# Two transformer blocks with expert layers: where the gate products stand in a round, and what ScalarE and VectorE do at the turn of a half

## The reference, cut to what matters

```python
def peer(x, w_q, sub_keys_1, sub_keys_2, u_tab, v_tab):
    ...
        q = (xb @ w_q).reshape(...)               # 8 heads, two parts each
        s1 = einsum('bthd,nd->bthn', q[..., 0, :], k1)   # 128 keys
        s2 = einsum('bthd,nd->bthn', q[..., 1, :], k2)   # 128 keys
        v1, i1 = top_k(s1, 16);  v2, i2 = top_k(s2, 16)
        top_s, pos = top_k(all sums of v1 and v2, 16)
        idx = i1 * 128 + i2 of those pairs        # one of 16384 experts
        g = softmax(top_s)
        h = einsum('bthkd,btd->bthk', u_tab[idx], xb)
        a = gelu(h) * g
        return einsum('bthk,bthkd->btd', a, v_tab[idx])
```

## Time and profile before

| | |
|---|---|
| median of 3 runs | 2250.28 us |
| the three runs | 2236.48, 2250.60, 2250.28 us |
| the profiled execution, its own time | 2250.24 us |
| its span in the profile | 2248.5 us |
| mean granted TensorE clock | 0.964 |
| PE busy | 2084.5 us, 93% |
| U stage, its gated half, block 1 | about 599 to 796 us |
| V stage, gated half, block 1 | about 800 to 1000 us |
| V stage, second half, block 1 | about 1008 to 1190 us |
| the same two turns in block 2 | at about 1840 and 2044 us |

### The profile page before, as it was taken

How to read it: one execution, slowest core, us unless ns; L and a number is a source line. 1 busy time by engine, 2 the same in 40 slices (tenths; PEclk the granted TensorE clock), 3 DMA queues, 4 the chain that set the end, 5 groups by cost and what they waited for, 6 DMA issues and landing times.

```text
span 2248.5 us, 41347 instructions
## 1 busy us (share of the span) xinstructions
PE 2084.5 (93%) x15340; PEld 1900.6 (85%) x15340; DVE 1239.6 (55%) x2076; ACT 976.5 (43%) x1206; POOL 1469.6 (65%) x592
## 2 busy tenths in 40 slices
PE   6898789998999999989997888999999999998997
PEld 6796789998999977768887868999999987776885
DVE  5547637992155556652334753996145556664333
ACT  3356344444444434434445453444444434443443
POOL 5654566798877767864445535699777768874442
PEclk9898899999999999999998989999999999999999
DMA  6332343444544444545555323445454445544553
GB/s 223 132 113 94 113 150 132 161 166 164 179 163 166 168 150 168 171 148 176 187 187 193 113 75 114 150 168 183 160 171 168 166 143 172 172 168 141 187 189 118
DMA packets 95823, 351.93 MB, mean 157 GB/s; under 512 B 11024, under 2 KB 11280, under 8 KB 95376
## 3 DMA queue, kind: packets, MB, share of 16 engines
q1 hardware_dynamic: 94752, 345.92, 45.9%
q10 hardware_dynamic: 1008, 5.13, 0.6%
HBM read 349.96 MB, written 1.05 MB: 156 GB/s over the span
## 4 chain that ended last, share of the span: by engine, by line
PE 76%; DVE 13%; POOL 4%; ACT 3%; issue 3%; DMA 1%; ACTq 0%; POOLq 0%; DVEq 0%; SPq 0%; PEldq 0%
PE ps L489 24%; PE ps L490 23%; PE ps L491 23%; POOL wlo L446 4%; PE ps L730 3%; DVE work L1347 1%; DVE work L1334 1%; PE ps L656 1%; DVE work L1327 1%; DVE work L1328 1%; DVE act L1171 1%; DVE whi L1103 1%; DVE act L1126 0%; DMA act<-in_const 0%; DVE act L1117 0%
## 5 line engine op out<-in xcount | busy, mean ns | idle before, releaser
L446 POOL TENSOR_TENSOR wlo<-ring,whi 128x1024 fp32r<-128x1024 f32 x588 | 1469.4, 2507 | 754.2 <-ACT whi L962 523.8
L962 ACT ACTIVATE whi<-ring 128x1024 fp32r<-128x1024 f32 x536 | 565.2, 1059 | 886.5 <-PE ps L491 841.2
L489 PE MATMUL ps<-hhi,whi 128*128 128x256 f32 x2432 | 701.1, 288 | 16.7 <-POOL wlo L446 15.3
L490 PE MATMUL ps<-hlo,whi 128*128 128x256 f32 x2432 | 692.2, 285 | 0.0
L491 PE MATMUL ps<-hhi,wlo 128*128 128x256 f32 x2432 | 691.8, 284 | 0.0
L489 PEld LDWEIGHTS ps<-hhi,whi 128*128 128x128 f32 x2432 | 471.3, 194 | 20.1 <-issue 11.6
L490 PEld LDWEIGHTS ps<-hlo,whi 128*128 128x128 f32 x2432 | 471.3, 194 | 0.0
L491 PEld LDWEIGHTS ps<-hhi,wlo 128*128 128x128 f32 x2432 | 470.7, 194 | 0.0
L489 PE MATMUL ps<-whi,shi 128*128 128x512 f32 x1024 | 413.8, 404 | 25.6 <-DVE slo L1430 25.6
L490 PE MATMUL ps<-wlo,shi 128*128 128x512 f32 x1024 | 408.6, 399 | 0.0
L491 PE MATMUL ps<-whi,slo 128*128 128x512 f32 x1024 | 407.6, 398 | 0.0
(11 more groups left out here) (241 smaller groups left out, 2029.3 us busy)
## 6 DMA issues: line engine op xcount, KB each, us to landing
ring<-in_weights SPq DMA_DIRECT2D x652, 512.0 KB, 3.3
act<-in_const SPq DMA_DIRECT2D x1, 2752.0 KB, 14.1
act<-in_const ACTq DMA_DIRECT2D x1, 2372.0 KB, 10.3
xres<-in_x SPq DMA_DIRECT2D x2, 512.0 KB, 4.4
act<-in_keys ACTq DMA_DIRECT2D x1, 1024.0 KB, 12.9
out<-act ACTq DMA_DIRECT2D x2, 512.0 KB, 2.6
act<-in_fgain ACTq DMA_DIRECT2D x1, 512.0 KB, 3.5
act<-in_keys SPq DMA_DIRECT2D x1, 128.0 KB, 13.8
```

The costliest lines, as they stand in the source:

```text
L446: pool.tensor_tensor(wlo[:, j, :], ring[:, j, :], whi[:, j, :].bitcast(F32), ALU.subtract)\
L489: pe.matmul(dst, wide[0], narrow[0], start=start, stop=False, skip_group_check=True)
L490: pe.matmul(dst, wide[0], narrow[1], start=False, stop=False, skip_group_check=True)
L962: eng.activation(whi[:, j, :], ring[:, j, :], ACT.Copy).then_inc(hi_ready[j], 1)
```

## The change

Three things. First, the gate products of a round follow tiles 0 and 2 (`EACH_GATED`), not 1 and 3; in the last round of each half they follow tiles 0 and 1 (`LAST_GATED`). Second, at the turn from U to V: ACT's last U round is written out, and `left(0, 0)` and `left(1, 1)` stand behind the rounding of place 2, ahead of the last gelu (now `open_pair(k, 2)`, which waits for `slot_used` of the last U tile) and of the rounding of place 3; DVE runs only one `hot` of the next half between the last two applies, and the other behind `rest_of(0, 0)` and `rest_of(1, 1)`; PE begins V's first tile with the second 128 tokens (t = 1, banks 2 and 3) and waits for the last gelu only ahead of t = 0. Third, in V's round 15 ACT's wait for `gates_used` of 64 stands behind the rounding of places 0 and 1, directly ahead of the `left` of pair 32. The sum that is computed is the same, and so is the number of all instructions but those of the waits and loops.

```diff
--- before.py
+++ after.py
@@ -72,6 +72,7 @@
 GATE_SCALE = 2.0 ** 14
 assert GROUPS == 2 * HALF_ROUND
 
+EACH_GATED, LAST_GATED = (0, 2), (0, 1)
 POOL_PLACES, DVE_PLACES = (0, 2), (1, 3)
 
 
@@ -731,14 +732,14 @@
                                            hot1[:, c, w, q, :], start=(q + w == 0), stop=(w == 1), skip_group_check=True)
                     mm.then_inc(n["gates_ready"], 1)
 
-                def u_round(k, first=False, gated=False):
+                def u_round(k, first=False, gate_after=()):
                     for j in range(RING):
                         pe.wait_ge(lo_ready[j], k + (first_u // RING + 1))
                         if j % 2 == 0 and not first:
                             pe.wait_ge(n["gelu_done"], k * 2 + (j // 2 - 1))
                         tile(j, bank(j // 2, (j % 2) * S, (j % 2 + 1) * S))
-                        if gated and j % 2:
-                            gates(k, -GROUPS, j // 2)
+                        if j in gate_after:
+                            gates(k, -GROUPS, gate_after.index(j))
 
                 u_round(0, first=True)
                 with pe.Fori(1, U_MID) as k:
@@ -753,31 +754,32 @@
                 mm.then_inc(n["selT_ready"], 1)
                 with pe.Fori(U_MID, HALF_ROUND) as k:
                     u_round(k)
-                u_round(HALF_ROUND, gated=True)
-                with pe.Fori(HALF_ROUND + 1, ROUNDS) as k:
-                    u_round(k, gated=True)
-
-
-                pe.wait_ge(n["gelu_done"], E_TILES // 2)
-
-                def v_round(k, first=False, last=False, gated=False):
+                u_round(HALF_ROUND, gate_after=EACH_GATED)
+                with pe.Fori(HALF_ROUND + 1, ROUNDS - 1) as k:
+                    u_round(k, gate_after=EACH_GATED)
+                u_round(ROUNDS - 1, gate_after=LAST_GATED)
+
+                def v_round(k, first=False, last=False, gate_after=()):
                     for j in range(RING):
                         pe.wait_ge(lo_ready[j], k + (first_v // RING + 1))
                         if j % 2 == 0:
                             pe.wait_ge(n["pair_ready"], k * 2 + (j // 2 + 1))
-                        for t in range(TT):
+                        for t in ((1, 0) if first and j == 0 else (0, 1)):
+                            if first and j == 0 and t == 0:
+                                pe.wait_ge(n["gelu_done"], E_TILES // 2)
                             for half in range(2):
                                 c, a = slice(half * 512, (half + 1) * 512), slice(t * P, (t + 1) * P)
                                 mm = split_product(bank(2 * t + half),
                                                    (shi[:, j // 2, j % 2, a], slo[:, j // 2, j % 2, a]),
                                                    (whi[:, j, c], wlo[:, j, c]), first and j == 0, last and j == RING - 1)
                         mm.then_inc(slot_used, 1)
-                        if gated and j % 2:
-                            gates(k, GROUPS, j // 2)
-
-                v_round(0, first=True, gated=True)
-                with pe.Fori(1, HALF_ROUND) as k:
-                    v_round(k, gated=True)
+                        if j in gate_after:
+                            gates(k, GROUPS, gate_after.index(j))
+
+                v_round(0, first=True, gate_after=EACH_GATED)
+                with pe.Fori(1, HALF_ROUND - 1) as k:
+                    v_round(k, gate_after=EACH_GATED)
+                v_round(HALF_ROUND - 1, gate_after=LAST_GATED)
                 with pe.Fori(HALF_ROUND, ROUNDS - 1) as k:
                     v_round(k)
                 v_round(ROUNDS - 1, last=True)
@@ -978,13 +980,16 @@
                                        bank(6 + (h - 1) % 2).rearrange("p (t c k) -> p t c k", t=TT, c=2), ACT.Copy)\
                            .then_inc(n["s_copied"], 1)
 
+                def open_pair(k, j):
+
+                    eng.activation(act[:, bass.ds(k * RING + j, 2), :], bank(j // 2).rearrange("p (e t) -> p e t", e=2),
+                                   gelu).then_inc(n["gelu_done"], 1)
+
                 def u_round(k):
                     for j in range(0, RING, 2):
                         high(first_u + j + RING, j, k)
                         high(first_u + j + 1 + RING, j + 1, k)
-
-                        eng.activation(act[:, bass.ds(k * RING + j, 2), :], bank(j // 2).rearrange("p (e t) -> p e t", e=2),
-                                       gelu).then_inc(n["gelu_done"], 1)
+                        open_pair(k, j)
 
                 def left(p, j):
 
@@ -998,23 +1003,32 @@
                 eng.activation(esel[:, :, 2, :, :].rearrange("p t h k -> p t (h k)"),
                                esel[:, :, 2, :, :].rearrange("p t h k -> p t (h k)"), ACT.Exp).then_inc(n["exp_ready"], 1)
                 eng.preload_act_table(gelu)
-                with eng.Fori(U_MID, ROUNDS) as k:
+                with eng.Fori(U_MID, ROUNDS - 1) as k:
                     u_round(k)
-
+                k = ROUNDS - 1
+                high(first_u + RING, 0, k)
+                high(first_u + 1 + RING, 1, k)
+                open_pair(k, 0)
+                high(first_u + 2 + RING, 2, k)
                 eng.wait_ge(n["gates_used"], GROUPS)
                 left(0, 0)
                 left(1, 1)
-
-                def v_round(k):
+                eng.wait_ge(slot_used, first_u + E_TILES)
+                open_pair(k, 2)
+                high(first_u + 3 + RING, 3, k)
+
+                def v_round(k, gated=0):
                     for j in range(RING):
                         high(first_v + j + RING, j, k)
+                        if j == 1 and gated:
+                            eng.wait_ge(n["gates_used"], gated)
                         if j % 2:
                             left(k * 2 + (2 + j // 2), j // 2)
 
                 with eng.Fori(0, HALF_ROUND - 1) as k:
                     v_round(k)
-                eng.wait_ge(n["gates_used"], 2 * GROUPS)
-                with eng.Fori(HALF_ROUND - 1, ROUNDS - 1) as k:
+                v_round(HALF_ROUND - 1, gated=2 * GROUPS)
+                with eng.Fori(HALF_ROUND, ROUNDS - 1) as k:
                     v_round(k)
                 split[0] = first_v + E_TILES
 
@@ -1421,7 +1435,7 @@
                 last_k = HALF_ROUND - 1
                 for c in range(2):
                     apply(last_k, c, 0, 0, c)
-                    hot(0, c, GROUPS, 1, c)
+                hot(0, 0, GROUPS, 1, 0)
                 eng.wait_ge(n["gates_used"], GROUPS)
 
                 def rest_of(p, j):
@@ -1438,6 +1452,7 @@
 
                 rest_of(0, 0)
                 rest_of(1, 1)
+                hot(0, 1, GROUPS, 1, 1)
                 eng.wait_ge(n["gelu_done"], E_TILES // 2)
                 with eng.Fori(0, HALF_ROUND - 1) as k:
                     for c in range(2):
```

## The result

The changed kernel takes 2215.32 us (median of 4 runs, 2208.03 to 2218.78) and the kernel before 2250.26. The ratio on record is 0.9864 with a 95% interval of 0.9819 to 0.9909; it is not the quotient of the two medians, which is 0.9845. By the medians the change takes 34.9 us less, where 32.8 were forecast (2217.4 us). Run to run, both kernels scatter by some 10 us. The profiles place it: PE starts on the first block's U tiles, after a wait for POOL, at 398.3 to 400.9 us in six of the thirteen profiled executions told of here and at 407.3 to 409.4 in the other seven, so most of the scatter comes from the first 400 us, which no edit here touches. Both kernels' main profiles are of the later kind (407.26 before, 409.02 after).

What follows compares the result with a forecast made beforehand. PE's own queue was taken to set the time, with gains only where PE stops at the turns. 22.0 (middle of V) + 10.8 (turn from U to V) = 32.8 us off 2250.2 gave 2217.4 us, range 2203 to 2228.

Steps and rivals of the forecast that it cites:

- The middle of V: Middle of V: PE's stop of 8.55 us and slow tile's 2.45 go, 11.0 us per block, 22.0 in all.
- The turn from U to V: Turn from U to V: PE's stop shrinks from 4.56 to 1.44 us, slow first tile goes; 10.8 us in two blocks.
- the step: At the turn, DVE's rest_of waits for POOL's low and ends at 4.27, so PE stands for 1.44 us.
- The clock: At the turn, PE's clock is kept after 1.44 us, winning 2.29; rival: it falls, 2222.0 us, chance 0.08.
- The lower bound of the middle's gain: Middle of V: at least 4.7 us won if a rest_of and one rounding stayed exposed and the clock fell.
- Gates after tiles 0 and 2: Inside the U and V halves: the earlier gates cost zero, as PE stays full.
- Almost no slack: Gated V rounds: DVE's loop just closes in one period of 6.07 us, yet rest_of is ready 1.8 ahead of PE.
- the slower rival: Gated V rounds: POOL takes the port twice running, PE stands 1.0 us each half round, 63 lost, 2280 us; chance 0.04.
- DVE's pace: Gated V rounds: DVE needs 6.36 us per half round, 0.29 over the period, 17.4 back, 2234.8 us; chance 0.06.
- No lock: At the turn, DVE gets its operands beside POOL, PE does not stand, 2 x 1.44 more won, 2214.5 us; chance 0.10.
- the middle in part: Middle of V: ACT holds a rounding back or a low waits, 4.7 us won of 11.0, 2230.0 us; chance 0.06.

Runs made afterwards that it cites:

- e1: The changed kernel with gates after tiles 1 and 3 again in all rounds except the last of each half; 2208.54 us, ratio to before 0.9841.
- e2: The changed kernel with the turn from U to V put back as in the kernel before, the middle of V staying changed; 2227.49 us, ratio 0.9913.
- e6: The changed kernel with ACT's wait for the last gates of V ahead of its whole round 15 again; 2222.98 us in one run.
- e7: The changed kernel with the gates of V's round 15 after tiles 1 and 3 again, ACT's wait staying as changed; 2210.0 us.
- e3: The changed kernel with ACT's gates wait and two pair roundings moved ahead of rounding weight place 2 in U's last round; 2207.18 us, ratio 0.9834.
- e4: The changed kernel with the low of weight place 2 at the turn made by DVE behind its two slo, not by POOL; 2214.86 us.
- e8: The changed kernel with two more DVE instructions of 0.60 us ahead of each gated one-hot of V; 2218.35 us in one run.
- e9: The changed kernel with four more DVE instructions of 0.60 us ahead of the one-hots in each gated V half round; 2268.41 us in one run.

## Why the prediction was right

**The bound.** PE's queue sets the time, and nothing inside a half was to be won: e1 shows it, and PE is full in 184 of 184 us.

**The middle of V, 22.0 us.** Shown. PE does not stop; e2 alone takes 12.2 + 11.0 = 23.2 us off the layers, 11.2 + 10.9 = 22.1 of them in V, where its edits are. The steps came as written: slo of pair 32 ended 3.25 us after the last gates' start (3.3 forecast) and that of pair 33 9.3 us after (9.1). What the prediction did not say is how the two edits share it; e6 and e7 do.

**The turn from U to V, 10.8 us.** The mechanism and nearly the size. PE stands for 1.60 us; the step put it at 1.44, since POOL began its low 1.40 after the end of tile 2 and not 1.33, and slo ended a little more behind it. The total difference to e2 is 3.6 + 6.8 = 10.4 us between the wide marks and 4.9 + 5.2 = 10.0 between the close ones, a little under the 10.8: the stop is 0.16 us longer than forecast, and the slow first tile took 4.84 us in e2's first block (791.56 to 796.40) and not 5.09, so there was less to win behind it. That POOL's instruction holds DVE's was read from one row of before; e3, e4 and e6 show it from three sides (slo moved, POOL's low removed, two of each made to meet).

**The clock.** Kept after 1.60 us, as taken; e6 and e7 add that it is kept after 2.93 and 2.82. The lower bound of the middle's gain had the clock fall for a stop of 3.9 us; no run stopped PE for a time between 2.93 and 4.56 at these turns, so that is open. The slow tiles behind the four stops are gone (2.87 us and not 5.09 at the turn).

**Gates after tiles 0 and 2, at no cost.** Right: 60 slo in the gated V rounds and the first at each turn took 2.3 to 2.4 us, DVE's time rose by 95.8 us, PE's did not. "Almost no slack" was too timid. e8 shows that another 1.2 us per half round fit, since a DVE that comes later waits less. A loss of about the size that the slower rival priced, 1.05 us per half round, does exist, and e9 shows it at 1.16. But it comes by the mechanism of the rival "DVE's pace", with about 2.4 us more DVE work; a POOL that takes its turn twice running was seen in none of the rows read here.

**The rivals.** "No lock" fell at the turn (1.60 us of stop and 2.99 us for two slo). "DVE's pace" and "the middle in part" left no stop to see. The mechanism was right, and that the median lies within 2 us of the forecast is in part luck, since whole runs scatter by 10. By layers it is 33.6 against 32.8, and in the stretches that the edits reach 32.1; the rest stands where nothing was edited.

**Which parts earn.** The last round's gates and ACT's order at the two turns: in the middle each was undone alone (e7, e6), at the turn from U to V only both together (e2), so how those two share their 10 us is not shown. The even places, the moved one-hot and the order of t are idle in this kernel; whether the last two would earn in e3, where PE comes sooner, was not tried.

## What to carry to other kernels

Where a long accumulation needs all of something before it can turn, look at the last round only: put its producers one or two tiles early and let the rest of the schedule be. Before moving a VectorE instruction with two SBUF inputs, lay GpSimd's instructions beside it: it costs its own length or about that plus the rest of GpSimd's, and an engine whose busy time is made of such waits is not full. To judge an edit worth 3 us in runs that scatter by 10, compare stretches between marks of the trace, and set the marks close around the edit.

## What the runs showed of the hardware

The granted clock of TensorE survived stops of 1.60, 2.82 and 2.93 us and was at its lower level behind stops of 4.56 and 8.55 us (0.51 to 0.52 of full speed over the first tile of before, 0.55 over that of e2, near whose end it had risen again). The stops up to 2.93 us cost only themselves; those of 4.56 us cost 2.0 to 2.3 us more.

The hold between POOL and DVE goes both ways and, in e6, by turns. slo took 0.68 us alone, 1.52 issued 1.4 us into POOL's low, 2.32 issued 0.6 into it and 2.83 when it had to wait for a low that had itself waited; POOL's low took 2.39 alone and 2.93 behind two slo (e3). That a VectorE instruction with two SBUF inputs and a GpSimd one that reads SBUF contend, and that the later issued one blocks, is what the Trainium skill states (SBUF — State Buffer, "Who interferes with whom"); the runs agree in both directions (2.32 beside 0.68, 2.93 beside 2.39).
